# A decoder trunk's six layer norms: the bias joins the scaling in one VectorE instruction ahead of the turn

## The chip, the cores and the metric

The kernel runs on one core of one Trainium2 chip. The metric is the device time of one execution in microseconds (us), smaller is better. The time before is 1612.59 us, the median of 3 runs (1611.76 to 1615.92).

## The reference, cut to what matters

Two layers, 512 tokens, width 1024, all in float32. Each layer has three sublayers (a token mixer, cross-attention into 256 memory tokens, a SwiGLU), and each ends in a layer norm of the residual, so there are six:

```python
def layer_norm(x, g, b):
    mu = jnp.mean(xf, axis=-1, keepdims=True)
    var = jnp.mean(jnp.square(xf - mu), axis=-1, keepdims=True)
    y = (xf - mu) * lax.rsqrt(var + LN_EPS)
    return y * g + b

for layer in range(2):
    x = layer_norm(ALPHA * x + mixer(x),            ln_g[layer, 0], ln_b[layer, 0])
    x = layer_norm(ALPHA * x + cross_attention(x),  ln_g[layer, 1], ln_b[layer, 1])
    x = layer_norm(ALPHA * x + swiglu(x),           ln_g[layer, 2], ln_b[layer, 2])
```

## The kernel before

**Layout.** The residual `x_res` is kept token-major: 4 tiles (t = 0 to 3) of 128 tokens x 1024 features. Products want their input feature-major, so behind every norm but the last TensorE turns the 8 blocks of 128x128 of each tile into PSUM ("the turn"), ScalarE copies them out rounded (`fm_hi`), and VectorE writes the rest of the precision (`fm_lo`). Each product is three passes (hi x hi, lo x hi, hi x lo, line 620). Norm (l, i) is that of layer l, sublayer i.

**Weights.** They come in chunks of 128 x 512 through a ring of 4 slots. For each chunk SyncE issues the DMA, ScalarE rounds it (`w_hi`, line 1008), GpSimd subtracts (`w_lo`, line 580), and TensorE uses it. SyncE may reload a slot once GpSimd has split the chunk in it; ScalarE may round into a slot once TensorE has used the chunk before it. The last 8 chunks of the product ahead of a norm are held in buffers of their own, so that this product can be finished token tile by token tile (one tile each 5.6 us), with the norm of a finished tile running beside the product of the next.

**The order around a norm** is written out by hand for each engine, with semaphores between them:

- TensorE: product ahead of the norm, tile by tile; in layer 0 then a product of the memory tokens (`v0_0`, `k1_0`, `v1_0`, the first filler); `turn_normed` (line 869); in layer 0 a second filler (`v0_1`, `k1_1`, `v1_1`), in layer 1 the first half of the next product (`early_half`, tokens of tiles 0 and 1). Both need the turned tiles 0 and 1 copied out by ScalarE and VectorE. PSUM is two halves of four banks, one half for two turned tiles, and tile 2 needs the half that the first filler used.
- VectorE, `norm` (line 1513), for each tile: add the second half of the product to the residual (line 1504), statistics (1509, 1545), variance + eps (1546), (x - mean) * g (1548), wait for ScalarE's square root, reciprocal (1551). Then the `fm_lo` parts (`turned_low`, recorded at line 1330), and last `bias` for four tiles (line 1554).
- ScalarE, `norm` (line 1126): square root (1143), scaling of the tile by the reciprocal (`scaled`, line 1147), which signals `x_ready`; then it rounds weight chunks, copies turned tiles (1032), empties the fillers (1124, 1037), and rounds on.

**The bias.** What is turned has no bias yet. Behind the four turns of each half tile TensorE adds it in PSUM by one more matmul (line 884), of a 16-row operand `bias_rows` (the bias split into two parts by three small VectorE instructions, lines 1523 to 1526) and a 0/1 selection `bias_sel`. `x_res` itself gets its bias later: by `bias` on VectorE, which signals `x_whole`; in the last norm by GpSimd for tiles 0, 1 and half of 2 (line 597) and by VectorE for the rest. SyncE waits for `x_whole` before it loads the next norm's parameters (lines 476 to 481) and before it stores the output (524 to 531); the next `add_residual` waits for it too (1503).

```python
dve: norm()    for t: add_second(t); stats; (x - mean) * g; reciprocal -> ln_coef
               for t: turned_low(t)
               for t: bias(t) -> x_whole
act: norm()    for t: scaled(t) -> x_ready; round_weights(...)
pe:  turn_normed()  for t: for half: 4 turns + 1 bias matmul -> tile_turned
```

Of the kernel before, what the change touches and what calls it, by code (L numbers as in the profile page):

```python
# [38 lines left out]
P = 128  # L39
# [37 lines left out]
C_SEL = C_ROWOK + TT  # L77
C_LOW = C_SEL + KT
C_END = C_LOW + 2
# [17 lines left out]
def shape_constants():  # L97

    c = np.zeros((P, C_END), np.float32)
    c[:, C_ID:C_ID + P] = np.eye(P)  # L100
    q, k = np.arange(P)[:, None], np.arange(P)[None, :]
    c[:, C_CAUSAL:C_CAUSAL + P] = np.where(k <= q, 0.0, NEG)
    for g, w in enumerate(WINDOWS):
        c[:, C_PINV + g * PAD:C_PINV + (g + 1) * PAD] = 1.0 / np.minimum(np.arange(PAD) + 1, w)
    c[:, C_INVF:C_INVF + HALF] = np.float32(500000.0) ** (-np.arange(HALF, dtype=np.float32) * np.float32(2.0) / np.float32(ROT))
    for t in range(TT):
        ends = np.arange(32) * CMP_STRIDE + CMP_BLOCK - 1
        tok = t * P + np.arange(P)
        c[:, C_CMASK + t * 32:C_CMASK + (t + 1) * 32] = np.where(ends[None, :] <= tok[:, None], 0.0, NEG)
        c[:, C_ROWOK + t] = tok >= CMP_BLOCK - 1  # L110
    row = np.arange(P)
    c[:, C_SEL:C_SEL + KT] = row[:, None] % KT == np.arange(KT)
    c[:, C_LOW] = row // KT % 2
    c[:, C_LOW + 1] = 1 - 2 * c[:, C_LOW]
    return c
# [78 lines left out]
def hybrid_trunk(nc, a, out):  # L194

    ctx = ExitStack()
    with ctx:
# [36 lines left out]
        bias_sel, _ = place("bias_sel", [2 * KT, KT], F32R)  # L234
        ln_g, o_ln = place("ln_g", [P, D], F32)
        ln_b, _ = place("ln_b", [P, D], F32)
        bias_raw, _ = place("bias_raw", [2 * KT, P], F32)
        bias_hi, _ = place("bias_hi", [2 * KT, P], F32R)
        bias_rows, _ = place("bias_rows", [2 * KT, P], F32R)
# [118 lines left out]
        ln_var, ln_sd, ln_coef, x_ready = sem("ln_var"), sem("ln_sd"), sem("ln_coef"), sem("x_ready")  # L358
        bias_ready, tile_turned = sem("bias_ready"), sem("tile_turned")
        x_whole, x_whole_pool = sem("x_whole"), sem("x_whole_pool")  # L360
# [90 lines left out]
        def _(sp):  # L451
# [53 lines left out]
            sp.wait_ge(x_whole, TT * 2)  # L505
# [3 lines left out]
            sp.wait_ge(x_whole, TT * 3)  # L509
# [7 lines left out]
            sp.wait_ge(x_whole, TT * 4)  # L517
            ln_params(1, 1)
            weights(CHUNK0["q1_1"], CHUNK0["up1_1"])
            sp.wait_ge(x_whole, TT * 5)  # L520
# [3 lines left out]
            for t in range(TT - 1):  # L524
                sp.wait_ge(x_whole_pool, t + 1)
                part = HALVES[0] if t == TT - 2 else slice(0, D)
                sp.dma_start(out[0, t * P:(t + 1) * P, part], x_res[:, t, part]).then_inc(s_out, 16)
            for n, (t, part) in enumerate(((TT - 2, HALVES[1]), (TT - 1, HALVES[0]), (TT - 1, HALVES[1]))):
                sp.wait_ge(x_whole, TT * (3 * DEPTH - 1) + n + 1)
                sp.dma_start(out[0, t * P:(t + 1) * P, part], x_res[:, t, part]).then_inc(s_out, 16)  # L530
            sp.wait_ge(s_out, 16 * (TT + 2))
# [34 lines left out]
        def _(pool):  # L566
# [34 lines left out]
        def _(pe):  # L601
# [240 lines left out]
            for l in range(DEPTH):  # L842
# [149 lines left out]
        def _(act):  # L992
# [133 lines left out]
            def norm(l, i, fillers=None):  # L1126
# [14 lines left out]
                def scaled(t):  # L1141
                    act.wait_ge(ln_var, TT * v + t + 1)
                    nc.scalar.activation(lnc[:, 1, t:t + 1], lnc[:, 0, t:t + 1], ACT.Sqrt).then_inc(ln_sd, 1)
                    act.wait_ge(ln_coef, TT * v + t + 1)

                    for part in HALVES if (l, i, t) == (DEPTH - 1, 2, TT - 1) else (slice(0, D),):
                        nc.scalar.activation(x_res[:, t, part], x_res[:, t, part], ACT.Copy, scale=lnc[:, 2, t:t + 1]).then_inc(x_ready, 1)

                for t in range(TT - 1):
                    scaled(t)  # L1150
# [3 lines left out]
                scaled(TT - 1)  # L1154
# [165 lines left out]
        def _(dve):  # L1320
# [18 lines left out]
            nc.vector.tensor_copy(bias_sel[:, :], consts[0:2 * KT, C_SEL:C_SEL + KT])  # L1339
# [173 lines left out]
            def norm(l, i, names):  # L1513
# [10 lines left out]
                rows = slice(0, 2 * KT)  # L1524
                settle(nc.vector.tensor_scalar(bias_raw[:, :], bias_raw[:, :], consts[rows, C_LOW:C_LOW + 1], None, ALU.mult))
                nc.vector.scalar_tensor_tensor(out=bias_rows[:, :], in0=bias_hi[:, :].bitcast(F32), scalar=consts[rows, C_LOW + 1:C_LOW + 2],
                                               in1=bias_raw[:, :], op0=ALU.mult, op1=ALU.add).then_inc(bias_ready, 1)
# [14 lines left out]
                for t in range(TT):  # L1542
# [13 lines left out]
                if (l, i) == (DEPTH - 1, 2):  # L1556
                    dve.wait_ge(x_ready, TT * v + TT - 1)
                    bias(TT - 2, HALVES[1])
                    for n, part in enumerate(HALVES):
                        dve.wait_ge(x_ready, TT * (v + 1) + n)  # L1560
                        bias(TT - 1, part)
                else:
# [212 lines left out]
```

## Time and profile before

| | |
|---|---|
| median of 3 runs | 1612.59 us |
| the profiled execution's own time | 1615.31 us |
| its span | 1613.4 us |
| TensorE busy | 1554.4 us (96%), mean granted clock 0.99 |
| VectorE, ScalarE, GpSimd busy | 560.4, 626.4, 678.1 us (35, 39, 42%) |
| DMA | 147.1 MB, mean 91 GB/s |
| chain that ended last | TensorE 88%, VectorE 5%, ScalarE 3%, GpSimd 3% |

Times in the profile are microseconds from the start of the span. PE is TensorE, PEld its weight loads, DVE VectorE, ACT ScalarE, POOL GpSimd, SP SyncE; L884 is line 884. "Idle before" is the time for which the engine waited ahead of an instruction, with what ended the wait. The six norms lie at about 300 to 337 us (0,0), 455 to 493 (0,1), 850 to 889 (0,2), 1085 to 1111 (1,0), 1218 to 1242 (1,1) and 1588 to the end (1,2).

### The profile page before, as it was taken

Reading aid. Unit: us, or ns where it says so; the run is one execution under the profiler, and the core shown is the slowest. Engines: PE = TensorE matmul, PEld = TensorE weight load, DVE = VectorE, ACT = ScalarE, POOL = GpSimd, SP = SyncE. Lnnn points to the kernel's source line nnn. Section 1 sums busy time; section 2 is a strip of 40 time slices with the busy share of each in tenths; the row PEclk is TensorE's granted clock in tenths of the full one; section 3 lists DMA queues with packets and bytes.
Section 4 is the critical chain, followed back from the end, with each engine's and each line's share of the span. In section 5 each row is a group of like instructions: output and inputs, shape, how many; then the busy total and the mean of one; then the engine's idle time right before and its main releaser. Section 6 shows DMA issues by size and latency. Waiting matters only on the chain.

```text
span 1613.4 us, 21392 instructions
## 1 busy us (share of the span) xinstructions
PE 1554.4 (96%) x7850; PEld 1284.5 (80%) x7850; DVE 560.4 (35%) x936; ACT 626.4 (39%) x1216; POOL 678.1 (42%) x517
## 2 busy tenths in 40 slices
PE   7999999999999999999999998899999999999998
PEld 7878988778787888888887776688878888888886
DVE  2742565442443111100013489955336101111013
ACT  3344544353434333333233366634443323333222
POOL 4452001463246444444453543353332544444444
PEclk9999999999999999999999999999999999999999
DMA  8431000343134333333232422332211333333232
GB/s 220 126 108 55 1 2 20 92 129 100 35 99 142 98 96 95 91 104 98 92 117 85 140 76 62 102 112 79 72 57 62 118 102 95 97 98 98 92 97 86
DMA packets 113601, 147.10 MB, mean 91 GB/s; under 512 B 20374, under 2 KB 69872, under 8 KB 113520
## 3 DMA queue, kind: packets, MB, share of 16 engines
q1 hardware_dynamic: 113200, 145.93, 30.5%
q8 instruction: 53, 0.87, 0.2%
q14 instruction: 28, 0.23, 0.0%
q0 software_dynamic: 320, 0.08, 0.0%
HBM read 143.86 MB, written 2.10 MB: 90 GB/s over the span
## 4 chain that ended last, share of the span: by engine, by line
PE 88%; DVE 5%; ACT 3%; POOL 3%; issue 1%; DMA 0%; SPq 0%; ACTq 0%; DVEq 0%
PE ps L620 76%; PE ps L821 3%; POOL w_lo L580 3%; PE ps L801 2%; PE ps L785 2%; PE ps L882 1%; PE ps L884 1%; PE ps L625 1%; PE ps L747 1%; PE ps L852 1%; ACT px L1267 1%; ACT w_hi L1008 0%; PE ps L777 0%; DVE tm L1632 0%; DVE a_sq L1628 0%
## 5 line engine op out<-in xcount | busy, mean ns | idle before, releaser
L580 POOL TENSOR_TENSOR w_lo<-w_raw,w_hi 128x512 fp32r<-128x512 f32 (+1 forms) x452 | 606.1, 1350 | 909.8 <-ACT w_hi L1008 908.0
L1008 ACT ACTIVATE w_hi<-w_raw 128x512 fp32r<-128x512 f32 (+1 forms) x452 | 278.3, 626 | 607.7 <-PE ps L620 553.1
L620 PE MATMUL ps<-fm_hi,w_hi 128*128 128x512 f32 (+1 forms) x1096 | 419.3, 383 | 10.8 <-ACT gelu L1170 6.3
L620 PE MATMUL ps<-fm_lo,w_hi 128*128 128x512 f32 (+1 forms) x1096 | 417.8, 381 | 0.0
L620 PE MATMUL ps<-fm_hi,w_lo 128*128 128x512 f32 (+1 forms) x1096 | 417.7, 381 | 0.0
L620 PEld LDWEIGHTS ps<-fm_hi,w_hi 128*128 128x128 f32 x1096 | 207.3, 189 | 52.6 <-ACT gelu L1170 7.2
L620 PEld LDWEIGHTS ps<-fm_lo,w_hi 128*128 128x128 f32 x1096 | 207.3, 189 | 39.4 <-issue 0.5
L620 PEld LDWEIGHTS ps<-fm_hi,w_lo 128*128 128x128 f32 x1096 | 207.3, 189 | 39.4
L1743 DVE TENSOR_TENSOR gf<-silu,ps 128x512 f32<-128x512 f32 x44 | 28.3, 684 | 420.7 <-ACT silu L1297 403.9
L1504 DVE SCALAR_TENSOR_TENSOR x_res<-x_res,ps 128x512 f32<-128x512 f32 x48 | 31.4, 685 | 313.5 <-PE ps L620 313.5
L620 PE MATMUL ps<-w_hi,g_hi 128*128 128x512 f32 x288 | 113.8, 395 | 0.0
L620 PE MATMUL ps<-w_hi,g_lo 128*128 128x512 f32 x288 | 113.8, 395 | 0.0
L620 PE MATMUL ps<-w_lo,g_hi 128*128 128x512 f32 x288 | 113.8, 395 | 0.0
L1330 DVE TENSOR_TENSOR fm_lo<-ps,fm_hi 128x512 fp32r<-128x512 f32 x68 | 43.1, 685 | 66.1 <-ACT fm_hi L1032 52.2
L620 PEld LDWEIGHTS ps<-w_hi,g_lo 128*128 128x128 f32 x288 | 54.0, 187 | 13.2
L620 PEld LDWEIGHTS ps<-w_hi,g_hi 128*128 128x128 f32 x288 | 54.0, 187 | 13.2
L620 PEld LDWEIGHTS ps<-w_lo,g_hi 128*128 128x128 f32 x288 | 54.0, 187 | 13.2
L620 PE MATMUL ps<-w_hi,fm_hi 128*128 128x512 f32 x160 | 62.6, 391 | 1.3 <-DVE fm_lo L1330 0.9
L620 PE MATMUL ps<-w_hi,fm_lo 128*128 128x512 f32 x160 | 62.3, 389 | 0.0
L620 PE MATMUL ps<-w_lo,fm_hi 128*128 128x512 f32 x160 | 62.3, 389 | 0.0
L1099 ACT ACTIVATE probs<-ps,negmax 128x31 f32<-128x31 f32 (+4 forms) x96 | 41.6, 450 | 48.8 <-DVE weight L1476 43.2
L821 PE MATMUL ps<-kv_tok,probsT 128*128 128x64 f32 x320 | 40.1, 278 | 1.6 <-DVE probsT L1471 1.5
(286 smaller groups left out, 2245.6 us busy)
## 6 DMA issues: line engine op xcount, KB each, us to landing
w_raw<-in_f_w_up SPq DMA_DIRECT2D x352, 128.0 KB, 2.1
w_raw<-in_f_w_down SPq DMA_DIRECT2D x88, 256.0 KB, 2.7
w_raw<-in_x_wkv SPq DMA_DIRECT2D x64, 256.0 KB, 3.2
w_raw<-in_o_w_in SPq DMA_DIRECT2D x40, 256.0 KB, 2.7
w_raw<-in_x_wq SPq DMA_DIRECT2D x32, 256.0 KB, 2.9
w_raw<-in_x_wo SPq DMA_DIRECT2D x32, 256.0 KB, 2.7
w_raw<-in_e_w_in SPq DMA_DIRECT2D x24, 256.0 KB, 3.0
w_raw<-in_o_w_out SPq DMA_DIRECT2D x20, 256.0 KB, 2.7
```

What stands on the lines that cost most here:

```text
L580: nc.gpsimd.tensor_tensor(lo[:, :n], w_raw[:, c % RING, :n], hi[:, :n].bitcast(F32), ALU.subtract).then_inc(w_split, 1)
L620: last = nc.tensor.matmul(outp, lhsT, rhs, start=(clear and k == 0 and n == 0), stop=(k == steps - 1 and n == 2), skip_group_check=True)
L625: return nc.tensor.transpose(out_, in_, ident[0:n, 0:n])
L747: nc.tensor.matmul(ps[0:NCMP, b0 + g, n * HD:(n + 1) * HD], src, cmp_w[half, n, l, :], start=(l == 0), stop=(l == CMP_BLOCK - 1))
L785: nc.tensor.matmul(ps[:, bank_, c0:c0 + m], q, k_[:, BRANCHES.index(b), g, :m], start=(i == 0), stop=False, skip_group_check=True)
L801: last = nc.tensor.matmul(ps[0:n, 4 + j // 4, jj * P:(jj + 1) * P], p, ident, start=True, stop=True, is_transpose=True if n == P else None)
L821: last = nc.tensor.matmul(ps[:, 6 + u % 2, r * HD:(r + 1) * HD], p, v, start=(i == mine[0][0]), stop=(i == mine[-1][0]))
L1008: nc.scalar.activation(w_pair(c)[0][:, :n], w_raw[:, s, :n], ACT.Copy).then_inc(w_rounded, 1)
L1099: last = nc.scalar.activation(probs_of(u, r)[:, :n], ps[:, 2 * (u % 2) + hh % 2, c0:c0 + n], ACT.Exp, bias=negmax[:, u % 2, r:r + 1], accu ...
L1330: nc.vector.tensor_tensor(lo, full, hi.bitcast(F32), ALU.subtract).then_inc(done, 1)
L1504: nc.vector.scalar_tensor_tensor(out=xs, in0=xs, scalar=ALPHA, in1=bank(name, t), op0=ALU.mult, op1=ALU.add).then_inc(evac_d, 1)
L1743: nc.vector.tensor_tensor(gf[:, j, :], silu[:, j, :], bank(name, 2 + j), ALU.mult).then_inc(evac_d, 1)
```

## The change

VectorE itself does the last step of the norm, x * (1 / sd) + b, in one instruction per tile (two halves for the very last tile), right behind the reciprocal; this now signals `x_ready`, and the tile is whole when it is turned. ScalarE keeps the square root alone (`scaled` becomes `deviation`). The bias matmuls, `bias_rows`, `bias_sel` and their preparation, the two small parameter DMAs of each norm, `bias` on VectorE and the additions on GpSimd go. All that waited for `x_whole` waits for `x_ready`. Tile 2 of the output is stored by one DMA in place of two.

```diff
@@ ln_params (SyncE)
                 sp.dma_start(ln_b[:, :], a["ln_b"][l, i].partition_broadcast(P)).then_inc(s_lnp, 16)
-                for half in (0, 1):
-                    sp.dma_start(bias_raw[half * KT:(half + 1) * KT, :],
-                                 a["ln_b"][l, i].rearrange("(k p) -> k p", p=P)).then_inc(s_lnp, 16)
@@ every wait for the whole residual (SyncE, add_residual)
-            sp.wait_ge(x_whole, TT * 1)
+            sp.wait_ge(x_ready, TT * 1)
...
@@ the output (SyncE)
-            for t in range(TT - 1):
-                sp.wait_ge(x_whole_pool, t + 1)
...
-            for n, (t, part) in enumerate(((TT - 2, HALVES[1]), (TT - 1, HALVES[0]), (TT - 1, HALVES[1]))):
...
+            for t in range(TT):
+                for n, part in enumerate(HALVES if t == TT - 1 else (slice(0, D),)):
+                    sp.wait_ge(x_ready, TT * (3 * DEPTH - 1) + t + n + 1)
+                    sp.dma_start(out[0, t * P:(t + 1) * P, part], x_res[:, t, part]).then_inc(s_out, 16)
@@ GpSimd
-            pool.wait_ge(s_lnp, 64 * 3 * DEPTH)
-            for t in range(TT - 1):
-                part = HALVES[0] if t == TT - 2 else slice(0, D)
-                pool.wait_ge(x_ready, TT * (3 * DEPTH - 1) + t + 1)
-                nc.gpsimd.tensor_tensor(x_res[:, t, part], x_res[:, t, part], ln_b[:, part], ALU.add).then_inc(x_whole_pool, 1)
@@ turn_normed (TensorE)
-                    pe.wait_ge(bias_ready, v + 1)
                     for t in range(TT):
                         if t % 2 == 0:
                             b0 = begin(f"ln{l}{i}_{t // 2}")
                         pe.wait_ge(x_ready, TT * v + t + 1)
                         for half in (0, 1):
-                            dst = ps[:, b0 + 2 * (t % 2) + half, :]
                             for kk in range(4):
                                 k = 4 * half + kk
-                                nc.tensor.matmul(dst[:, kk * P:(kk + 1) * P], x_res[:, t, k * P:(k + 1) * P], ident,
-                                                 start=(kk == 0), stop=False, is_transpose=True, skip_group_check=True)
-                            last = nc.tensor.matmul(dst.rearrange("p (k s) -> p k s", s=P), bias_rows[:, :],
-                                                    bias_sel[:, 4 * half:4 * half + 4].unsqueeze(2).to_broadcast([2 * KT, 4, P]),
-                                                    start=False, stop=True, skip_group_check=True)
+                                last = turn(ps[:, b0 + 2 * (t % 2) + half, kk * P:(kk + 1) * P], x_res[:, t, k * P:(k + 1) * P])
                         last.then_inc(tile_turned, 1)
@@ norm (ScalarE)
-                def scaled(t):
+                def deviation(t):
                     act.wait_ge(ln_var, TT * v + t + 1)
                     nc.scalar.activation(lnc[:, 1, t:t + 1], lnc[:, 0, t:t + 1], ACT.Sqrt).then_inc(ln_sd, 1)
-                    act.wait_ge(ln_coef, TT * v + t + 1)
-
-                    for part in HALVES if (l, i, t) == (DEPTH - 1, 2, TT - 1) else (slice(0, D),):
-                        nc.scalar.activation(x_res[:, t, part], x_res[:, t, part], ACT.Copy, scale=lnc[:, 2, t:t + 1]).then_inc(x_ready, 1)
@@ norm (VectorE)
-                dve.wait_ge(s_lnp, 64 * (v + 1))
-                settle(nc.vector.tensor_copy(bias_hi[:, :], bias_raw[:, :]))
...
+                dve.wait_ge(s_lnp, 32 * (v + 1))
@@
                     dve.wait_ge(ln_sd, TT * v + t + 1)
-                    nc.vector.reciprocal(lnc[:, 2, t:t + 1], lnc[:, 1, t:t + 1]).then_inc(ln_coef, 1)
-
-                def bias(t, part=slice(0, D)):
-                    nc.vector.tensor_tensor(x_res[:, t, part], x_res[:, t, part], ln_b[:, part], ALU.add).then_inc(x_whole, 1)
...
+                    settle(nc.vector.reciprocal(lnc[:, 2, t:t + 1], lnc[:, 1, t:t + 1]))
+                    for part in HALVES if (l, i, t) == (DEPTH - 1, 2, TT - 1) else (slice(0, D),):
+                        nc.vector.scalar_tensor_tensor(out=x_res[:, t, part], in0=x_res[:, t, part], scalar=lnc[:, 2, t:t + 1],
+                                                       in1=ln_b[:, part], op0=ALU.mult, op1=ALU.add).then_inc(x_ready, 1)
+
+                if (l, i) != (DEPTH - 1, 2):
                     for t in range(TT):
                         turned_low(t)
-                    for t in range(TT):
-                        bias(t)
                     whole[0] += TT
```

The constants of `bias_sel` leave the constant tile, and the memory of the removed tiles is kept as a gap of 64 bytes, so that what lies behind stays where it was.

## Rows read from the trace of the kernel before

**Rows 1.** The page: busy time of the engines.
```profile
PE 1554.4 (96%) x7850; PEld 1284.5 (80%) x7850; DVE 560.4 (35%) x936; ACT 626.4 (39%) x1216; POOL 678.1 (42%) x517
```

**Rows 2.** Chain of waits, four stretches: start us, us, engine, what.
```profile
338.36 10.20 POOL w_lo L580 x5
...
494.02 10.21 POOL w_lo L580 x5
...
890.36 10.21 POOL w_lo L580 x5
...
1118.67 4.27 POOL w_lo L580
...
1167.31 0.89 PE ps L625 x8
```

**Rows 3.** TensorE by line: count | busy us, mean ns.
```profile
L884 PE MATMUL ps<-bias_sel,bias_rows 16*128 16x512 f32 x40 | 19.1, 478 | 0.0
```

**Rows 4.** Timeline of TensorE, norm (0,0): start us, us.
```profile
321.77 0.40 PE L620 MATMUL ps<-w_lo,mem_hi 128*128 128x512 f32 x1
322.96 0.50 PE L620 MATMUL ps<-w_hi,mem_hi 128*128 128x512 f32 x1 [0.79 <-POOL w_lo L580]
...
328.66 0.60 PE L882 MATMUL ps<-consts,x_res 128*128 128x128 f32 x4
...
336.57 0.50 PE L620 MATMUL ps<-w_hi,mem_hi 128*128 128x512 f32 x1
...
350.10 0.39 PE L620 MATMUL ps<-fm_hi,w_hi 128*128 128x512 f32 x1
```

**Rows 5.** Timeline of ScalarE, VectorE and GpSimd, norm (0,0).
```profile
319.88 1.15 ACT L1147 ACTIVATE x_res<-x_res,lnc 128x1024 f32<-128x1024 f32 x1 [1.19 <-DVE lnc L1551]
...
331.33 1.29 DVE L1330 TENSOR_TENSOR fm_lo<-ps,fm_hi 128x512 fp32r<-128x512 f32 x2 [11.49 <-ACT fm_hi L1032]
...
338.51 8.89 DVE L1554 TENSOR_TENSOR x_res<-x_res,ln_b 128x1024 f32<-128x1024 f32 x4
...
321.63 7.68 POOL L580 TENSOR_TENSOR w_lo<-w_raw,w_hi 128x512 fp32r<-128x512 f32 x6 [4.30 <-ACT w_hi L1008]
```

**Rows 6.** Timeline of VectorE, norm (1,0), last token tile and what follows it.
```profile
1102.70 0.69 DVE L1504 SCALAR_TENSOR_TENSOR x_res<-x_res,ps 128x512 f32<-128x512 f32 x1 [2.35 <-PE ps L620]
...
1104.47 1.28 DVE L1548 SCALAR_TENSOR_TENSOR x_res<-x_res,mv,ln_g 128x1024 f32<-128x1024 f32 x1
1105.82 0.16 DVE L1551 RECIPROCAL lnc<-lnc 128x1 f32<-128x1 f32 x1
...
1112.35 4.62 DVE L1554 TENSOR_TENSOR x_res<-x_res,ln_b 128x1024 f32<-128x1024 f32 x4
```

**Rows 7.** Timeline of TensorE, norm (1,0): end of the turn, and the first wait behind it.
```profile
1110.41 0.39 PE L620 MATMUL ps<-fm_hi,w_hi 128*128 128x256 f32 x1
...
1122.99 0.50 PE L620 MATMUL ps<-fm_hi,w_hi 128*128 128x512 f32 x1 [0.81 <-POOL w_lo L580]
```

**Rows 8.** Timeline of VectorE, end of the last norm.
```profile
1608.65 0.17 DVE L1551 RECIPROCAL lnc<-lnc 128x1 f32<-128x1 f32 x1
...
1609.60 1.31 DVE L1554 TENSOR_TENSOR x_res<-x_res,ln_b 128x512 f32<-128x512 f32 x2 [0.20 <-ACT x_res L1147]
```

**Rows 9.** TensorE by stretches: us, busy us (instructions), granted clock, DMA share, GB/s.
```profile
7.00:12.70 5.70, 5.62 (x27) 1.00 1.05 367
12.70:16.10 3.40, 1.25 (x11) 1.00 0.55 220
16.10:19.50 3.40, 3.40 (x19) 0.51 0.58 155
156.00:166.30 10.30, 10.30 (x49) 0.50 0.01 5
```

**Rows 10.** Timeline of TensorE: the last turns of the input, and the first matmul behind.
```profile
12.80 0.71 PE L625 MATMUL ps<-consts,x_res 128*128 128x128 f32 x5
15.67 0.35 PE L620 MATMUL ps<-fm_hi,w_hi 128*128 128x256 f32 x1 [2.15 <-ACT fm_hi L1032]
```

More of the change, by code:

```diff
@@ L76 @@
 C_ROWOK = C_CMASK + TT * 32
-C_SEL = C_ROWOK + TT
-C_LOW = C_SEL + KT
-C_END = C_LOW + 2
+C_END = C_ROWOK + TT
 V_POSK, V_POSV = 0, CMP_BLOCK
@@ L110, in shape_constants @@
         c[:, C_ROWOK + t] = tok >= CMP_BLOCK - 1
[L111 to L114, printed above, removed]
     return c
@@ L233, in hybrid_trunk @@
         lru_c, _ = place("lru_c", [P, 2, RT], F32)
-        bias_sel, _ = place("bias_sel", [2 * KT, KT], F32R)
+        cur[0] += 64
         ln_g, o_ln = place("ln_g", [P, D], F32)
         ln_b, _ = place("ln_b", [P, D], F32)
-        bias_raw, _ = place("bias_raw", [2 * KT, P], F32)
-        bias_hi, _ = place("bias_hi", [2 * KT, P], F32R)
-        bias_rows, _ = place("bias_rows", [2 * KT, P], F32R)
         cur[0] = o_ln + 10 * 2 * P * 4
@@ L355, in hybrid_trunk @@
         x_turned, x_rounded, x_split = sem("x_turned"), sem("x_rounded"), sem("x_split")
-        ln_var, ln_sd, ln_coef, x_ready = sem("ln_var"), sem("ln_sd"), sem("ln_coef"), sem("x_ready")
-        bias_ready, tile_turned = sem("bias_ready"), sem("tile_turned")
-        x_whole, x_whole_pool = sem("x_whole"), sem("x_whole_pool")
+        ln_var, ln_sd, x_ready = sem("ln_var"), sem("ln_sd"), sem("x_ready")
+        tile_turned = sem("tile_turned")
         g_hi_ready, g_ready = sem("g_hi_ready"), sem("g_ready")
@@ L501, in _ @@
             weights(CHUNK0["ein3"], CHUNK0["q0_1"])
-            sp.wait_ge(x_whole, TT * 1)
+            sp.wait_ge(x_ready, TT * 1)
             ln_params(0, 1)
             weights(CHUNK0["q0_1"], CHUNK0["up0_1"])
-            sp.wait_ge(x_whole, TT * 2)
+            sp.wait_ge(x_ready, TT * 2)
             ln_params(0, 2)
@@ L508, in _ @@
             weights(CHUNK0["dn0_0"], CHUNK0["oin1"])
-            sp.wait_ge(x_whole, TT * 3)
+            sp.wait_ge(x_ready, TT * 3)
             sp.dma_start(w_gates[:, 0, :, :], a["o_wa"][0].rearrange("h i j -> i h j")).then_inc(s_wgates, 16)
@@ L516, in _ @@
             weights(CHUNK0["oout0"], CHUNK0["q1_1"])
-            sp.wait_ge(x_whole, TT * 4)
+            sp.wait_ge(x_ready, TT * 4)
             ln_params(1, 1)
             weights(CHUNK0["q1_1"], CHUNK0["up1_1"])
-            sp.wait_ge(x_whole, TT * 5)
+            sp.wait_ge(x_ready, TT * 5)
             ln_params(1, 2)
@@ L523, in _ @@
             weights(CHUNK0["dn1_0"], len(CHUNKS))
-            for t in range(TT - 1):
-                sp.wait_ge(x_whole_pool, t + 1)
-                part = HALVES[0] if t == TT - 2 else slice(0, D)
-                sp.dma_start(out[0, t * P:(t + 1) * P, part], x_res[:, t, part]).then_inc(s_out, 16)
-            for n, (t, part) in enumerate(((TT - 2, HALVES[1]), (TT - 1, HALVES[0]), (TT - 1, HALVES[1]))):
-                sp.wait_ge(x_whole, TT * (3 * DEPTH - 1) + n + 1)
-                sp.dma_start(out[0, t * P:(t + 1) * P, part], x_res[:, t, part]).then_inc(s_out, 16)
-            sp.wait_ge(s_out, 16 * (TT + 2))
+            for t in range(TT):
+                for n, part in enumerate(HALVES if t == TT - 1 else (slice(0, D),)):
+                    sp.wait_ge(x_ready, TT * (3 * DEPTH - 1) + t + n + 1)
+                    sp.dma_start(out[0, t * P:(t + 1) * P, part], x_res[:, t, part]).then_inc(s_out, 16)
+            sp.wait_ge(s_out, 16 * (TT + 1))
         def group_filled(eng, name):
@@ L591, in _ @@
             split(done, len(CHUNKS))
-            pool.wait_ge(s_lnp, 64 * 3 * DEPTH)
-            for t in range(TT - 1):
-                part = HALVES[0] if t == TT - 2 else slice(0, D)
-                pool.wait_ge(x_ready, TT * (3 * DEPTH - 1) + t + 1)
-                nc.gpsimd.tensor_tensor(x_res[:, t, part], x_res[:, t, part], ln_b[:, part], ALU.add).then_inc(x_whole_pool, 1)
         @block.tensor
@@ L1139, in turned_copies @@
                         copy_turned(f"ln{l}{i}_{t // 2}", fm_hi, 2 * (t % 2) + j)
-                def scaled(t):
+                def deviation(t):
                     act.wait_ge(ln_var, TT * v + t + 1)
                     nc.scalar.activation(lnc[:, 1, t:t + 1], lnc[:, 0, t:t + 1], ACT.Sqrt).then_inc(ln_sd, 1)
-                    act.wait_ge(ln_coef, TT * v + t + 1)
-                    for part in HALVES if (l, i, t) == (DEPTH - 1, 2, TT - 1) else (slice(0, D),):
-                        nc.scalar.activation(x_res[:, t, part], x_res[:, t, part], ACT.Copy, scale=lnc[:, 2, t:t + 1]).then_inc(x_ready, 1)
                 for t in range(TT - 1):
-                    scaled(t)
+                    deviation(t)
                     round_weights(following + (1, 3, 4)[t])
@@ L1153, in norm @@
                     turned_copies(0)
-                scaled(TT - 1)
+                deviation(TT - 1)
                 if fillers:
@@ L1338, in _ @@
             nc.vector.tensor_copy(ident_b[:, :], consts[:, C_ID:C_ID + P]).then_inc(tables_ready, 1)
-            nc.vector.tensor_copy(bias_sel[:, :], consts[0:2 * KT, C_SEL:C_SEL + KT])
             nc.vector.tensor_copy(causal_b[:, :], consts[:, C_CAUSAL:C_CAUSAL + P]).then_inc(tables_ready, 1)
@@ L1502, in add_residual @@
                 if whole[0]:
-                    dve.wait_ge(x_whole, whole[0])
+                    dve.wait_ge(x_ready, whole[0])
                 nc.vector.scalar_tensor_tensor(out=xs, in0=xs, scalar=ALPHA, in1=bank(name, t), op0=ALU.mult,
@@ L1520, in norm @@
                     half_stats(0, names[0], t)
-                dve.wait_ge(s_lnp, 64 * (v + 1))
-                settle(nc.vector.tensor_copy(bias_hi[:, :], bias_raw[:, :]))
[L1524 to L1527, printed above, removed]
+                dve.wait_ge(s_lnp, 32 * (v + 1))
                 def turned_low(t):
@@ L1550, in norm @@
                     dve.wait_ge(ln_sd, TT * v + t + 1)
-                    nc.vector.reciprocal(lnc[:, 2, t:t + 1], lnc[:, 1, t:t + 1]).then_inc(ln_coef, 1)
-                def bias(t, part=slice(0, D)):
-                    nc.vector.tensor_tensor(x_res[:, t, part], x_res[:, t, part], ln_b[:, part], ALU.add).then_inc(x_whole, 1)
[L1556 to L1562, printed above, removed]
+                    settle(nc.vector.reciprocal(lnc[:, 2, t:t + 1], lnc[:, 1, t:t + 1]))
[3 more added lines that the diff above has]
+                if (l, i) != (DEPTH - 1, 2):
                     for t in range(TT):
                         turned_low(t)
-                    for t in range(TT):
-                        bias(t)
                     whole[0] += TT
```

## The prediction

> **What bounds the kernel now.** I read the page first: TensorE is busy 96% of the span, the other engines 35 to 42% [rows 1]. So time is lost or won only in what TensorE executes and where it stands. Then TensorE by line: the bias matmuls are 40, one per half tile, with a mean of 478 ns [rows 3]; these durations overlap their neighbours, so I don't add them up but take the distance between starts. Then the chain of waits, where it leaves TensorE near a norm: each time to GpSimd's `w_lo` [rows 2], the low part of a weight chunk. The timelines of the engines there say why.
>
> In norm (0,0) there are three losses. **First**, TensorE issued a matmul of the filler `v0_0` at 321.77 (pace 0.23 us) and the next at 322.96 [rows 4]: 0.96 us lost. GpSimd began the chunk only at 321.63, having waited for ScalarE to round it, and ScalarE rounds behind its scaling of tile 3 (319.88, 1.15 us) [rows 5]. **Second**, the turn of 32 blocks with 8 bias matmuls takes from 328.66 to 336.57 [rows 4], 7.91 us. **Third**, `v0_1` runs from 336.57 to 350.10 [rows 4], 13.53 us, though its 48 matmuls at 0.233 us want 11.2: 2.3 us lost. In that time GpSimd gave 5 chunks in 10.20 us [rows 2], 2.04 each, against 6 in 7.68, 1.28 each, at 321.63 [rows 5]. What ran beside them is VectorE's `bias`, 4 in 8.89 us, 2.2 each [rows 5]; with GpSimd idle the same four take 4.62 [rows 6], 1.16 each. Two SBUF additions on the two engines take turns, and TensorE pays. Norms (0,1) and (0,2) repeat it, with 10.21 us for 5 chunks each [rows 2].
>
> In layer 1 there is no filler. TensorE turns tile 0 while VectorE is still at tile 3, and the first matmul of the next product starts at 1110.41 [rows 7]. Behind norm (1,0) TensorE waits once more, to 1122.99 [rows 7], for a chunk for which GpSimd needed 4.27 us in place of 1.28 [rows 2]: VectorE was splitting the memory keys and values beside it, pushed late by `bias` (1112.35, 4.62 us) [rows 6].
>
> **The change, part by part.**
>
> *Bias matmuls out.* Turns alone: 8 in 0.89 us [rows 2], so 32 in 3.56 instead of 7.91. TensorE executes 4.35 us less per turned norm, five of them, 21.8 us in all. Not all of it arrives.
>
> *Scaling moved to VectorE.* The new instruction has the form of line 1548 (two SBUF inputs, one pointer scalar, 1024 elements): 1.28 us [rows 6]. Bounds: 1.16, the bare addition [rows 6], and 2.3, the addition beside GpSimd [rows 5]. I take 1.28, the same operation. It fits: in a tile VectorE is idle 2.35 us before the next [rows 6], and keeps about 1.0. At the upper bound it just fits. For the last tile of a layer 1 norm the chain is now reciprocal at 1105.82 + 0.16, a settle of 0.05, + 1.28 = 1107.3 [rows 6], where ScalarE's scaling ended before at about 1107.2: no loss. But VectorE's `turned_low` now starts behind it. Four tiles of 1.29 [rows 5]: tile 0 to 1108.6, tile 1 to 1109.9, and TensorE's next product needs both. It starts at 1109.95 instead of 1110.41: **0.45 us** gained, of 4.35. TensorE stands 1.9 us before the turn of tile 3 and 1.5 behind it. Twice, in (1,0) and (1,1): 0.9.
>
> *Layer 0, up to the second filler.* ScalarE no longer waits 1.19 us for the reciprocal and scales tile 3 for 1.15 [rows 5], rounds some 2.2 us earlier, and the 0.96 us wait goes (the new VectorE instruction can hold GpSimd up by at most its 1.28 there, less than the 2.2). The filler ends at 327.7, turns end at 331.3. Next late is the copying out: ScalarE empties `v0_0` (to 328.9), copies tile 0, VectorE's low parts run 329.5 to 332.1 (two tiles of 1.29), and `v0_1` starts at 332.15, 0.85 behind the turns. Gain 0.96 + 4.35 - 0.85 = **4.45**.
>
> *`bias` out.* Beside `v0_1` GpSimd has the port to itself: 1.28 per chunk against TensorE's 1.40. The first of these chunks can be rounded when tile 3 is copied, about 333.4, and is split by 335.4; TensorE wants it at 336.4. The reloads start with the splits and so come earlier too. The 2.3 us go: 4.45 + 2.3 = 6.7 for (0,0) and (0,2), 6.5 for (0,1), which has four short copies in front of the turned ones. **Three norms: 19.9.** Behind (1,0) the keys and values are split 4.6 us earlier, off GpSimd's chunk: the 0.81 us wait and 0.2 of restart go, **1.0**.
>
> *End.* Before: reciprocal at 1608.65, then scaling and addition by halves, to 1609.60 + 1.31 = 1610.91 [rows 8]. Now two halves of 0.69 behind the reciprocal: 1610.25. **0.65.** The halved output DMA of tile 2 isn't last.
>
> *At nothing:* 12 small parameter DMAs on SP's queue and three tiny VectorE instructions per norm, covered by TensorE's products (uncovered, some 0.3 us each); waits for `x_ready` in place of `x_whole`, which come earlier.
>
> *The clock.* In the new layer 1 norms TensorE has 0.9 us of turns in 4.9. The rows show what follows such a stretch: 1.25 us of work in 3.4, then the granted clock at 0.51, the 1.2 GHz level, for 3.4 us with TensorE busy [rows 9], after a wait of 2.15 [rows 10]. That costs half of the slow work, up to 1.7. I take one of the two places to fall, 1.3 us lost; bounds 0 and 3.4.
>
> Sum: 19.9 + 0.9 + 1.0 + 0.65 - 1.3 = **21.1 us**. The span goes from 1613.4 to 1592.3, the profiled execution from its own 1615.31 to 1594.2. The median shown lies 2.7 below that execution; I take the same gain off it: 1612.59 - 21.1 = **1591.5**.
>
> **A rule to weigh.** During the turns of the input TensorE went from 0.21 us a turn (27 in 5.7 us) [rows 9] to 0.11 from 12.80 on (5 turns) [rows 10], with no other work than turns: they seem to have brought the fast pace, though 367 GB/s of DMA beside the slow ones leaves a doubt, and the row prints 1.00 for both. The Trainium skill, "TensorE: Matmul & The Clock Gate", section Part 4, says that a transpose does not count as busy time of the engine as a matmul does. By that rule the removed matmuls were what held the clock; it is a rival below.
>
> **Rivals.**
>
> *A. Turns alone don't hold the clock.* Then it falls in each layer 0 norm as well (3.56 us of turns + 0.85 of wait), and in both of layer 1. Five times 1.7 instead of 1.3: 7.2 us less, **1598.7**. For it: none of the five turns of before, which all mix in matmuls, is followed by a fall. Against it: the pace above. Chance 0.12.
>
> *B. Weight supply stays late.* If GpSimd's 2.04 is not the `bias` but the pace of reloads, `v0_1` and its like keep their 2.3, and being earlier wait more: 3 x 2.3 + 1.0 less, and up to 0.96 x 3 more, 7.9 to 10.8, **1599 to 1602**. Against it: 1.28 per chunk at 321.63 with the same reloads. Chance 0.08.
>
> *C. All of TensorE's work arrives:* 5 x 4.35, plus the waits 0.96 x 3, 2.3 x 3, 1.0 and 0.65, is 33, **1579.5**. It needs VectorE's low parts off the way, where the sum has them last. Chance 0.02.
>
> *D. Slower.* One mechanism: the clock, falling in all five norms and staying low under the sparse start of what follows. It decides from 44 us of slow work, 9 in each norm, upwards (22 us of gain used up). The longest low stretch in the trace is 10.3 us [rows 9], under sparse attention; at that length it costs 5.15 x 5 = 25.8 against 22.4: **1616**. Against it: dense products follow each norm, and under these it was low for 3.4 us. Chance 0.02.
>
> *E. VectorE's instruction at 2.3 us* (its two SBUF inputs against GpSimd's): last tiles later by 1.0 in (1,0), (1,1) and the end, 3 less, **1594.5**; inside my range. Chance 0.1.
>
> **How the numbers follow.** My forecast has 0.66. Its unknown costs are clock (+1.3 to -2.1), E (-3) and the drift between executions (1611.8 to 1615.9 before). The range reaches from 1588.0 to 1599.5, which takes in A and E and the near end of B. About 0.3%, 4.8 us, is what a measurement of this kernel can tell from no change; every case but D is beyond it: faster 0.96, same 0.02 (a mixture of A and B with more late chunks), slower 0.02.
>
> **What would show it.** TensorE's turn of four tiles in layer 0 in 3.6 us; the next filler 0.9 behind it; `w_lo` at 1.3 us in these stretches and no wait of TensorE for it from 321 to 350; VectorE's new line at 1.28; the layer 1 products start 0.5 earlier, with two waits of 1.9 and 1.5; granted clock 0.5 behind at most two norms. Wrong it would be if chunks still came at 2 us without `bias`, or if the clock fell behind the pure turns of layer 0.

## The result and the profile after

| | before | changed |
|---|---|---|
| median (runs) | 1613.49 us (4) | 1598.03 us (4) |
| ratio, 95% interval | | 0.9891 (0.9872 to 0.991) |
| profiled execution, its span | 1615.31, 1613.4 | 1599.29, 1597.5 |
| TensorE busy, granted clock | 1554.4, 0.989 | 1535.8, 0.986 |
| VectorE, ScalarE, GpSimd busy | 560.4, 626.4, 678.1 | 556.9, 598.1, 669.5 |

By the ratio the change saves 17.6 us (14.5 to 20.7), by the two medians 15.5; 21.1 were forecast. The spans of the two traces differ by 15.9. Nearly all that was forecast inside the norms of layer 0 and at the end is there; what is missing went to TensorE's clock and the start.

**Layer 0.** Timeline of TensorE in the changed kernel, norm (0,0), against [rows 4]:

```profile
328.62 3.66 PE L604 MATMUL ps<-consts,x_res 128*128 128x128 f32 x32
...
333.18 0.47 PE L599 MATMUL ps<-w_hi,mem_hi 128*128 128x512 f32 x1 [0.90 <-ACT fm_hi L1005]
...
344.45 0.39 PE L599 MATMUL ps<-fm_hi,w_hi 128*128 128x512 f32 x1
```

The 32 turns take 3.66 us in place of 7.91 with the bias matmuls. The second filler starts 4.56 us behind the first turn, 0.90 of it a wait for the copies, and runs 11.27 us in place of 13.53. ScalarE, VectorE and GpSimd in the same stretch, against [rows 5]:

```profile
320.90 2.00 DVE L1517 SCALAR_TENSOR_TENSOR x_res<-x_res,lnc,ln_b 128x1024 f32<-128x1024 f32 x1
330.59 4.88 DVE L1299 TENSOR_TENSOR fm_lo<-ps,fm_hi 128x512 fp32r<-128x512 f32 x8 [7.69 <-ACT fm_hi L1005]
...
319.62 0.62 ACT L981 ACTIVATE w_hi<-w_raw 128x512 fp32r<-128x512 f32 x1
...
320.31 10.14 POOL L564 TENSOR_TENSOR w_lo<-w_raw,w_hi 128x512 fp32r<-128x512 f32 x7 [4.09 <-ACT w_hi L981]
334.57 10.74 POOL L564 TENSOR_TENSOR w_lo<-w_raw,w_hi 128x512 fp32r<-128x512 f32 x8 [4.11 <-ACT w_hi L981]
```

ScalarE rounds right behind its square root. The new instruction (line 1517) takes 2.00 us, not 1.28. GpSimd's seven low parts from 320.31 on are not all slowed by it. By line and stretch (mean ns of one behind the comma), the first, the second, and the other five:

```profile
L564 POOL TENSOR_TENSOR w_lo<-w_raw,w_hi 128x512 fp32r<-128x512 f32 x1 | 1.5, 1505 | 4.1 <-ACT w_hi L981 4.1
L564 POOL TENSOR_TENSOR w_lo<-w_raw,w_hi 128x512 fp32r<-128x512 f32 x1 | 2.3, 2279 | 0.0
L564 POOL TENSOR_TENSOR w_lo<-w_raw,w_hi 128x512 fp32r<-128x512 f32 x5 | 6.3, 1291 | 0.1
```

The second low part starts at 321.78, in the middle of VectorE's instruction (320.90 to 322.90), and ends 1.16 us behind it. So the two engines take turns by whole instructions: this tile costs VectorE 0.7 us and GpSimd 1.2 (0.2 and 1.0), and TensorE doesn't wait for either. The eight low parts beside the second filler, from 334.57 on, take 1.30 each.

**Layer 1.** TensorE at the end of the turn, norm (1,0), against [rows 7]:

```profile
1090.31 1.09 PE L604 MATMUL ps<-consts,x_res 128*128 128x128 f32 x8 [2.02 <-DVE x_res L1517]
1092.74 0.55 PE L599 MATMUL ps<-fm_hi,w_hi 128*128 128x256 f32 x1 [1.35 <-ACT fm_hi L1005]
1093.10 0.42 PE L599 MATMUL ps<-fm_lo,w_hi 128*128 128x256 f32 x1
1093.31 0.42 PE L599 MATMUL ps<-fm_hi,w_lo 128*128 128x256 f32 x1
```

TensorE waits 2.02 us for tile 3 and 1.35 behind it (the row names ScalarE's copy of tile 3; what the product needs is VectorE's low part of tile 1, out at 1092.60). Then the matmuls start 0.21 us apart instead of 0.12: the clock fell. By stretches (us, busy, granted clock, DMA share, GB/s):

```profile
1085.50:1092.70 7.20, 3.87 (x33) 0.96 0.23 91
1092.70:1096.10 3.40, 3.35 (x18) 0.58 0.52 186
1225.40:1228.80 3.40, 3.38 (x16) 0.52 0.52 187
```

It fell at both norms, (1,0) and (1,1), to the 1.2 GHz level.

**End.** VectorE's last instructions in the changed kernel, against [rows 8]:

```profile
1593.61 1.41 DVE L1517 SCALAR_TENSOR_TENSOR x_res<-x_res,lnc,ln_b 128x512 f32<-128x512 f32 x2
```

VectorE finishes 1593.61 + 1.41 = 1595.02, 4.69 behind the last residual addition (1590.33); before 1610.91 - 1605.57 = 5.34. That is the 0.65.

**The account of the 15.9 us,** from distances between the residual addition of tile 3 in one norm and the next, read from both traces' VectorE timelines:

| stretch | before | changed | saved | forecast |
|---|---|---|---|---|
| start to norm (0,0) | 316.61 | 317.62 | -1.0 | 0 |
| (0,0) to (0,1), (0,1) to (0,2) | 155.58, 396.43 | 149.02, 389.89 | 13.1 | 13.2 |
| (0,2) to the matmul behind the second filler's chain | 43.37 | 36.73 | 6.6 | 6.7 |
| on to (1,0) | 190.71 | 192.44 | -1.7 | 0 |
| (1,0) to (1,1) | 131.65 | 132.66 | -1.0 | 1.5, less the clock |
| (1,1) to (1,2) | 371.22 | 371.97 | -0.75 | 0.45, less the clock |
| (1,2) to the end | 7.86 | 7.15 | 0.7 | 0.65 |

### The profile page after: what moved, and what is told of

The parts are those of the page before. It is cut to its first block, busy times and chain, and to the rows that moved or that the text cites. A ratio compares the mean times of both kernels' runs of the same rounds, so it can differ in the third digit from the quotient of the medians.

```text
span 1597.5 us, 21249 instructions
## 1 busy us (share of the span) xinstructions
PE 1535.8 (96%) x7810; PEld 1283.6 (80%) x7810; DVE 556.9 (35%) x919; ACT 598.1 (37%) x1191; POOL 669.5 (42%) x514
## 4 chain that ended last, share of the span: by engine, by line
PE 87%; DVE 6%; ACT 4%; POOL 1%; DMA 1%; issue 1%; SPq 0%; DVEq 0%; ACTq 0%
PE ps L599 77%; PE ps L800 3%; PE ps L780 2%; PE ps L764 2%; POOL w_lo L564 1%; PE ps L604 1%; PE ps L726 1%; PE ps L831 1%; ACT fm_hi L1005 1%; ACT px L1236 1%; DMA w_raw<-in_x_wkv 1%; PE ps L756 0%; DVE tm L1588 0%; DVE a_sq L1584 0%; ACT w_hi L981 0%
## 5 line engine op out<-in xcount | busy, mean ns | idle before, releaser
L599 PEld LDWEIGHTS ps<-w_lo,g_hi 128*128 128x128 f32 x288 | 54.0, 188 | 13.2
L599 PEld LDWEIGHTS ps<-w_hi,g_hi 128*128 128x128 f32 x288 | 54.0, 188 | 13.2
L599 PEld LDWEIGHTS ps<-w_hi,g_lo 128*128 128x128 f32 x288 | 54.0, 188 | 13.1
L1116 ACT ACTIVATE lnc<-lnc 128x1 f32<-128x1 f32 x24 | 4.9, 203 | 115.6 <-DVE lnc L1510 115.6
```

The source lines that it names most:

```text
L599: last = nc.tensor.matmul(outp, lhsT, rhs, start=(clear and k == 0 and n == 0), stop=(k == steps - 1 and n == 2), skip_group_check=True)
```

## The experiments

Times are medians; "by the trace" means the distances of the table above. A "fall" is a stretch in which the granted clock is at its lower level, 1.2 GHz. "Idle matmuls" are matmuls put in to keep TensorE busy; their results are overwritten.

**The changed kernel once more, and the kernel before once more.** No edit.

> The changed kernel once more. In the first trace three things beyond the sum stood against it: the input tile landed 1.4 us later (8.48 against 7.08), the granted clock was at half level under 1.8 us more of the recurrence, and it was at half level for 3.4 us in the cross-attention of layer 1 (24 matmuls in 4.63 us against 3.09). Theory 1 (these three are the luck of an execution, the falls behind the two layer 1 norms are not): this run shows the clock at 0.5 at the start of the products behind both layer 1 norms again, in the cross-attention only perhaps, and the median lies 15 to 19 us under the kernel before. Rival (the falls behind the norms are chance too): one or both are missing, and that span is 1.4 us shorter for each. The parts that hang on no clock repeat within 0.1: layer 0 from the last residual addition of the norm to the end of the second filler 26.9 us (33.5 before), end of the kernel 7.2 us behind the last such addition (7.8 before).

> The kernel before once more, for a second profile of it. Five traces of other kernels agree on three stretches in which the first trace of before had less work at the half clock: 8 gate matmuls of the recurrence in 6.3 to 6.7 us (5.18 there), 336 matmuls behind the recurrence in 80.4 to 80.7 us (79.97), and the 24 matmuls of the cross-attention in layer 1 in 4.6 us (3.09). Theory 1 (that was luck; the clock's phase differs from execution to execution): this trace shows at least two of the three at the others' values. Rival (it belongs to the kernel): 5.2, 80.0 and 3.1 again, and the change has a cost of some 3 us outside the norms. In both, the turned norms show no fall of the clock, and layer 0 takes 33.5 us from the last residual addition to the end of the second filler.

Measured: 1596.84 us, ratio 0.9891 (0.9866 to 0.9916). Span 1592.8: the start took 312.34 instead of 317.62, with the clock at the lower level for 6.8 us of it instead of 17. It fell behind both layer 1 norms again. The kernel before: 1616.04 (one run), span 1614.2. The chain of waits of the two, first the changed kernel, then before:

```profile
962.06 6.61 PE ps L831 x8
...
1000.18 80.71 PE ps L599 x336
...
1141.89 4.62 PE ps L599 x24
```

```profile
986.66 5.18 PE ps L852 x8
...
1023.40 79.99 PE ps L620 x336
...
1164.88 3.14 PE ps L620 x24
```

The three stretches repeat in each kernel (first traces: 6.41, 80.57, 4.63 and 5.18, 79.97, 3.09). So "luck of an execution" is wrong for them: 3.4 us of the gain in the first pair of traces and 3.6 in the second are lost outside the norms, in code that the change doesn't touch. The landing of the input at the start, 6.5 to 8.5 us over all traces and 8.48 and 7.95 in this kernel, is luck. The falls behind the norms aren't.

**Only the late additions left out.**

```diff
-                    for t in range(TT):
-                        bias(t)
+                    dve.wait_ge(x_ready, TT * (v + 1))
+                    for t in range(TT):
+                        nc.vector.memset(lnc[:, 3, t:t + 1], 0.0).then_inc(x_whole, 1)
```

> The kernel before, with only the late additions of the bias to the residual left out in the five turned norms (so the residual carries no bias). This is the contention part alone. Theory 1 (the additions and GpSimd's low parts hold each other up on their way to SBUF): GpSimd's low parts beside the second fillers take 1.3 us instead of 2.04, TensorE doesn't wait there, 2.3 us less in each of three norms, and 1.0 less behind norm (1,0): 7.9 us faster than before, 1605.6. The 0.96 us wait in the first fillers stays. Rival (the low parts come at the pace of the reloads): 2.0 us each as before and no change, 0 to 1 us.

Measured: 1611.05 us, ratio 0.9973 (0.9956 to 0.999), 4.4 us saved. GpSimd by line between 338 and 352 us, first of the kernel before, then of this one from 330 to 352:

```profile
L580 POOL TENSOR_TENSOR w_lo<-w_raw,w_hi 128x512 fp32r<-128x512 f32 x8 | 13.9, 1776 | 7.5 <-ACT w_hi L1008 7.5
```

```profile
L580 POOL TENSOR_TENSOR w_lo<-w_raw,w_hi 128x512 fp32r<-128x512 f32 x8 | 10.2, 1297 | 8.0 <-ACT w_hi L1008 7.8
```

The same 8 chunks take 1.30 us each. Before, the mean of 1.78 was made of four at 1.29 and four at 2.26, the four that met an addition. TensorE doesn't wait in the second fillers now. By the trace it saves 2.16, 2.13 and 2.24 in the norms of layer 0 and 1.06 behind (1,0): 7.6, against 7.9 expected. Contention is shown; the reloads are not the bound. The whole kernel shows less because it, too, meets the clock at other places (8 gate matmuls in 6.70 us, the 336 in 80.68, 24 of the cross-attention in 4.65): 3.8 us more than before, though nothing of layer 1's turns was changed.

**Only the bias matmuls left out.**

```diff
-                                nc.tensor.matmul(dst[:, kk * P:(kk + 1) * P], x_res[:, t, k * P:(k + 1) * P], ident,
-                                                 start=(kk == 0), stop=False, is_transpose=True, skip_group_check=True)
-                            last = nc.tensor.matmul(dst.rearrange("p (k s) -> p k s", s=P), bias_rows[:, :], ...
+                                last = turn(dst[:, kk * P:(kk + 1) * P], x_res[:, t, k * P:(k + 1) * P])
```

> The kernel before, with only the bias matmuls of the turn left out (so what is turned has no bias). ScalarE still scales, VectorE still adds the bias late. Theory 1: a layer 0 turn goes from 7.91 us to 3.56, and of the 4.35 the copying out of tiles 0 and 1 takes 0.9 back: 3.5 each, 10.4 in three; the late additions start earlier by about 1.5 and still meet GpSimd's low parts, so 2.3 us of waits stay in each second filler, perhaps 1 more. In layer 1 VectorE's low parts are ahead of the turn there (they don't stand behind a scaling of VectorE's own), so the next product starts as soon as tile 3 is scaled, turned and copied, 1 to 2 us earlier than before, minus up to 1.7 if the clock falls. Together 9 to 13 us faster than before. Rival (TensorE's turn was hidden by something else): under 5 us.

Measured: 1603.03 us, ratio 0.9933 (0.9914 to 0.9953), 10.8 us saved; 9 to 13 were expected. By the trace 3.46 and 3.63 between the norms of layer 0 and 3.48 behind (0,2), 3.5 expected. GpSimd's low parts still take turns with the additions (10 chunks at 1744 ns, additions at 2125). From (1,1) to (1,2) it takes 369.82, 1.4 less than before and 2.15 less than the changed kernel. Of these 2.15, 0.72 is the product's earlier start, 6.33 behind the last addition instead of 7.05: here ScalarE scales tile 3, and VectorE's low parts don't stand behind a scaling of its own. The rest, 1.4, is the clock. TensorE's first matmuls behind norm (1,0), then behind (1,1), each with the third matmul after it:

```profile
1097.61 0.38 PE L620 MATMUL ps<-fm_hi,w_hi 128*128 128x256 f32 x1 [0.76 <-ACT fm_hi L1028]
...
1098.21 0.41 PE L620 MATMUL ps<-fm_hi,w_hi 128*128 128x256 f32 x1
```

```profile
1229.81 0.36 PE L620 MATMUL ps<-fm_hi,w_hi 128*128 128x256 f32 x1 [0.76 <-ACT fm_hi L1028]
...
1230.24 0.28 PE L620 MATMUL ps<-fm_hi,w_hi 128*128 128x256 f32 x1
```

Behind (1,0) the granted clock was 0.50 for 3.4 us, behind (1,1) it stayed at 1.00, though both norms have the same two waits, 1.90 and 0.76 us, and the same turns. With waits as short as these it can fall or hold; what decides between the two stays open.

In layer 0 the halves of the change are nearly independent: 6.5 for the additions and 10.6 for the bias matmuls. To the 19.7 measured, 2.6 are missing, 0.8 to 1.0 per norm. That is ScalarE's queue by the rows of the kernel before (0.96 lost ahead of the turn); no experiment took that piece alone.

**TensorE kept busy in layer 1.**

```diff
+                        if following and t == TT - 1:
+                            busy(i, ps[:, b0 + 2, :], 8)
                         pe.wait_ge(x_ready, TT * v + t + 1)
...
+                        pe.wait_ge(evac_d, DVE_BEFORE[name] + 2)
+                        busy(i, ps[:, 4 * (INDEX[name] % 2), :], 5)
                         evacuated(f"ln{l}{i}_0")
```

> The changed kernel with idle matmuls in the two layer 1 norms: 8 of 128x512 ahead of the turn of tile 3 (1.9 us, where TensorE waits 2.0) into the banks of tile 3, and 5 (1.2 us) into the banks of tile 0, once it is copied out, where it waits 1.35. Their results are overwritten. Theory 1 (the fall behind these norms comes from TensorE's two waits): the clock stays at 1.00 there, the first 16 matmuls of the next product go at 0.12 us instead of 0.21, 1.4 us less per norm, 2.8 us faster than the changed kernel, or 2 if the added work runs over by 0.4. Rival (something else lowers the clock, or it falls anyway): clock 0.5 again and 0 to 1 us slower than the changed kernel.

Measured: 1594.87 us, ratio 0.9874 (0.9848 to 0.99). That is 2 to 3 us below the changed kernel's two medians, but the intervals overlap, so the reading rests on the trace. TensorE by stretches over both norms:

```profile
1088.00:1094.80 6.80, 6.42 (x47) 1.00 0.45 154
1219.00:1226.00 7.00, 6.60 (x46) 1.00 0.40 152
```

No fall. From (1,1) to (1,2) 370.56 instead of 371.97, 1.41 less, and from (1,0) to (1,1) 131.44 instead of 132.66, 1.22 less: 2.6 for the two falls. The waits lowered the clock; the turns didn't.

**Every turn of layer 0 twice.**

```diff
-                            for kk in range(4):
+                            for kk in list(range(4)) * (1 if l else 2):
```

> The changed kernel with every turn of layer 0 done twice into the same bank: 64 turns in a row, with no other work of TensorE. Theory 1 (turns hold the clock as matmuls do; what lowered it in layer 1 was waiting): granted clock 1.00, 64 turns in 7.2 us (0.111 each), the second fillers start 3.6 us later less the 0.9 us wait for the copies, which is now covered in part: 3 x 3 to 3.6, some 10 us slower than the changed kernel. Rival (a transpose does not count as busy time, as the Trainium skill says in TensorE: Matmul & The Clock Gate, Part 4): the clock falls to 0.5 in each of the three stretches and the matmuls behind them go at half speed, 15 us slower or more.

Measured: 1605.59 us (one run). The chain of waits has the 64 turns, and the stretches show the clock:

```profile
873.38 6.99 PE ps L604 x64
```

```profile
328.00:335.20 7.20, 7.20 (x66) 1.00 0.39 129
335.20:339.00 3.80, 3.80 (x18) 1.00 0.00 0
479.00:486.30 7.30, 7.30 (x68) 1.00 0.59 178
```

7 us of nothing but turns, at the full level, and full speed behind them, in all three places. So these transposes, of 128x128 float32, hold the clock. The Trainium skill, "TensorE: Matmul & The Clock Gate", Part 4, says that a transpose doesn't count as busy time in the same way and that the full clock doesn't engage for it. This trace doesn't agree, and the measurement decides.

The second filler starts 17.9 to 18.1 us behind the last addition instead of 15.6 to 15.7, so the doubled turns cost 2.3 to 2.4 us in each of the three norms. From (0,1) to (0,2) it is 392.27 against 389.89, the 2.4. From (0,0) to (0,1) it is 152.89 against 149.02, 3.9, since there the clock also fell in the cross-attention of layer 0 (granted clock 0.51 from 398.6 to 402.0), where none of the other kernels' did. The three stretches behind, with the change in place, are near those of the kernel before (5.45, 80.02 and 3.09).

**Another order in layer 1.**

```diff
 # TensorE, ahead of the turn of tile 3
+                            evacuated(f"ln{l}{i}_0")
+                            early_half(following, 0, RING // 2)
 # VectorE, tile 3, ahead of (x - mean) * g
+                    if early:
+                        turned_low(0)
+                        turned_low(1)
```

> The changed kernel with another order in the two layer 1 norms: VectorE splits the turned tiles 0 and 1 as soon as the variance of tile 3 is out, ahead of its two long instructions on tile 3; TensorE starts the next product's first half (2 of 4 chunks) as soon as these are out, turns tile 3 then, and goes on. Theory 1 (the next product waits for VectorE's low parts, and for these alone): it starts 4.6 us behind the last residual addition instead of 7.0, tile 3 is ready in the middle of it, so TensorE waits once, 1.9 us, and gains 2.4 - 0.9 for the turn, 1.5 us per norm; if the clock also holds, 1.4 more: 3 to 6 us faster than the changed kernel, 1592 to 1594 beside its 1597. Rival (tile 3 becomes late in its place): TensorE waits behind the second chunk for its scaling, by up to 1.3, and the gain is under 2 us in all.

> The reordered kernel once more, beside the shifted one on one chip. Theory 1 (its gain over the changed kernel is 3.2 us per layer 1 norm, of which 1.7 from the order and 1.4 from a clock that does not fall): the distance from the last residual addition of norm (1,1) to that of (1,2) is 368.7 again (371.97 in the changed kernel), no fall of the clock at either norm, median 1588 to 1591. Rival (the clock held by chance): a fall at one of the norms or in the cross-attention, and 1.4 us more for each.

Measured: 1589.54 us, ratio 0.9837 (0.9814 to 0.986), and again 1588.57, ratio 0.9841 (0.9823 to 0.986): 26 us under the kernel before and some 8 under the changed one. TensorE's timeline and its chain:

```profile
1087.50 0.36 PE L599 MATMUL ps<-fm_hi,w_hi 128*128 128x256 f32 x1 [1.75 <-ACT fm_hi L1007]
1087.69 0.28 PE L599 MATMUL ps<-fm_lo,w_hi 128*128 128x256 f32 x1
```

```profile
1087.50 3.11 PE ps L599 x24
1090.60 0.87 PE ps L604 x8
1091.47 41.32 PE ps L599 x216
```

The product starts 4.34 us behind the last addition (1083.16), not 7.04, tile 3 is turned in its middle without a wait, and the clock holds. From (1,1) to (1,2) it takes 368.71 in both: 3.26 less than the changed kernel, 1.41 of it the clock, 1.85 the order. The cross-attention doesn't meet a fall in either trace, which gives 1.5 more.

**The same with 6 idle matmuls in the remaining wait.**

```diff
+                            busy(i, ps[:, b0 + 2, :], 6)
                             evacuated(f"ln{l}{i}_0")
```

> The order of the experiment before, and 6 idle matmuls of 128x512 (1.4 us, into the banks of tile 3) in the one wait that it leaves. Theory 1 (what is left of the fall comes from this wait): clock 1.00 in both norms; if it fell in the experiment before, 1.4 us per fall faster than that, if not, the same within 0.5. Rival: the matmuls push the product back, 0.2 to 0.5 slower per norm.

Measured: 1591.05 us, ratio 0.9844 (0.9818 to 0.987). From (1,1) to (1,2) 368.71: the same. There was nothing left to hold.

**The changed kernel shifted by 2.8 us.**

```diff
+                if l == 0:
+                    begin("dn0_0")
+                    for _ in range(12):
+                        nc.tensor.matmul(ps[:, 4 * (INDEX["dn0_0"] % 2), :], fm_hi[:, 0, 0:P], fm_hi[:, 0, :], start=True, stop=True)
                 product(f"dn{l}_0", (g_hi, g_lo), SEQ, False,
```

> The changed kernel with 12 idle matmuls of 128x512 (2.8 us of TensorE's time) ahead of the last product of layer 0, which shift all that follows by 2.8 us and change nothing else. In two traces each, the changed kernel had its clock rise 5.5 and 5.9 us behind the start of the second gate matmuls of the recurrence (8 in 6.4 and 6.6 us), the kernel before 2.9 in both (8 in 5.18). Theory 1 (some 3.3 us of the gain are given back outside the norms because an earlier kernel meets the clock's falls at other places; shifted by 2.8 it meets them where the kernel before does): 8 gate matmuls in 5.2 to 5.4, the 336 behind in 80.0, the 24 of the cross-attention in 3.1, so 3.3 gained for 2.8 spent: the same as the changed kernel within 1.5 us. Rival (what was given back belongs to the change itself): 6.4, 80.6 and 4.6 as in the changed kernel, and 2.8 us slower than it, 1600.

Measured: 1599.9 us, ratio 0.9896 (0.9881 to 0.991). The chain of waits:

```profile
969.01 5.13 PE ps L831 x8
...
1005.85 79.88 PE ps L599 x336
...
1147.85 4.27 PE ps L599 x24
1152.12 1.30 PE ps L604 x8
```

Half right. The recurrence is back at the values of the kernel before (5.13 and 79.88), so its 2 us belong to where the falls lie and not to the change. The doubled turns and the kernel without additions say the same: one has the change without these losses, the other the losses without most of the change. The cross-attention still met a fall (24 matmuls and 8 turns, 5.57 us against 3.98), and behind the layer 1 norms it stayed at the lower level for 6.8 us each, where it had been 3.4, for 1.2 us more from (1,0) to (1,1) (133.85) and 0.6 more from there to (1,2) (372.60). By the medians it is 1.9 to 3.1 us slower than the changed kernel, for 2.8 spent: what the recurrence gave, the norms took. The clock's share outside the norms can be moved, but no rule for it came out of this.

## Why the prediction was right or wrong

- **Right: the bound and the three losses of layer 0.** 19.9 forecast, 19.7 measured. Two pieces were run apart: additions out 2.2 per norm (2.3), matmuls out 3.5 (3.5). The third, ScalarE's queue, is what is left, 0.8 to 1.0 (0.96). The second filler starts 0.90 behind the turns (0.85). One reading on the way was a mean: the 2.04 us of a low part are one of 1.28 and four of 2.26.
- **Right: in layer 1 most of the 4.35 us less of TensorE's work becomes waiting.** The two waits are 2.02 and 1.35 (1.9 and 1.5). The product started 7.04 behind the last addition, 0.67 earlier than before (0.45). The wait for the chunk behind (1,0) is gone (1.0).
- **Right: the end,** 0.65 by VectorE's last instruction (0.65).
- **A size off without effect: VectorE's instruction.** I took 1.28 us. Beside GpSimd it takes 2.00, and VectorE keeps 0.32 us before the next tile, not 1.0. For tile 3 in layer 1, where GpSimd is idle, it is 1.28. Rival E, at 2.3, was near for the tiles where it costs nothing, and its 3 us didn't come.
- **Wrong: the clock in layer 1.** The step was "one of the two places to fall, 1.3 us lost". Both fall, in all four traces of kernels with this order in layer 1 (the changed one twice, turns doubled, shifted), and keeping TensorE busy gave back 1.22 and 1.41: 2.6 in place of 1.3. So the change is worth nothing in layer 1: 0.9 + 1.0 forecast before the clock, 2.3 measured, 2.6 given back. One of two falling is what the kernel without bias matmuls showed, with a second wait of 0.76 us instead of 1.35.
- **Missing: the clock elsewhere.** The sum had no term for stretches that the change doesn't touch. There 3.4 and 3.6 us were lost in the two pairs of traces: 1.8 and 2.1 in the recurrence, 1.5 in the cross-attention. The remaining 1.0 of the first pair is the start, where traces differ by more than that anyway.
- **The rivals.** A is refuted as a mechanism: the clock is 1.00 behind 32 turns in the changed kernel and behind 64 in the doubled one. The measured 1598.0 is near A's 1598.7 by chance. B is refuted: 1.30 us a chunk without the additions. C and D didn't come: VectorE's low parts were in the way, and the falls behind the changed kernel's norms lasted 3.4 us.

The 1598.0 lies inside the range near its upper end. That is partly luck: the upper end was there for A and B, which didn't come, and the clock, which took 6.0 us in the norms and elsewhere, stood in the sum at 1.3.

## What to carry to other kernels

Work taken from the busiest engine is worth what the next wait leaves of it: 21.8 us of matmuls removed alone gave 10.8, and where no filler stood by, the work turned into waits behind which the clock fell. Order the work so that such a wait goes, rather than fill it: putting VectorE's low parts and the next product's start ahead of tile 3 gave 3.3 us per norm (1.4 of it the clock), idle matmuls 1.4 at most. And an addition on VectorE with both inputs in SBUF isn't free beside a GpSimd stream that feeds TensorE, even where VectorE itself has time: four of them cost TensorE 2.2 us in each norm of layer 0. It isn't always paid by TensorE: the new instruction held GpSimd up by 1.2 us a tile at most, and TensorE didn't wait for it.

## What of the hardware I had not expected

- VectorE's long instruction and GpSimd's low parts wait for each other's running instruction: 2.00 instead of 1.28 us for the one, 1.51 and then 2.28 instead of 1.28 for the others. The same form a step earlier (line 1512) keeps its 1.28 us, since GpSimd's chunk starts only in its last 0.35 us; it is the chunk that waits then, the 0.2 in its 1.51.
- A run of short VectorE instructions keeps GpSimd out to its end. Before, behind norm (1,0), GpSimd's low part began at 1118.67 [rows 2] in the middle of VectorE's eight subtractions for the memory keys and values (0.69 us each, the last one done at 1121.80), and ended at 1122.93, 1.13 behind them: 4.26 us instead of 1.28. Against the longer additions of `bias` the two engines alternated.
- From the recurrence on, the falls of the clock lie at the same places in both traces of the kernel before and in both of the changed one (8 gate matmuls in 5.18 and 5.18 us, 6.41 and 6.61); at the start they differ. Changes elsewhere in the kernel move them, at a cost here of some 2 us in the recurrence and 1.5 in the cross-attention. Why they keep to the kernel was not tried; that a shift alone moves them, one experiment showed for the recurrence.
